# The first projection takes X before its norm; its units are scaled per token when they leave PSUM, and seven convolution taps go from VectorE to TensorE

## The chip, the cores and the metric

The kernel runs on one core of a Trainium2 chip, as one program with one launch. The metric is the device time in microseconds (us) of one execution; the time before is the median of three. The engines are TensorE (PE; its weight loads are PEld), VectorE (DVE), ScalarE (ACT), GpSimd (POOL) and SyncE (SP, which here only issues transfers). Each engine works through its own list of instructions in order and waits on semaphores.

## The reference

Two transformer blocks over 512 tokens of width 1024 in float32. The change lies in the first mixer of the first block. Its part of the reference, cut:

```python
def rmsnorm(x, g):
    y = x32 * lax.rsqrt(jnp.mean(x32 * x32, axis=-1, keepdims=True) + EPS)
    return (y * g).astype(x.dtype)

def conformer_conv(h, w_pw1, b_pw1, w_dw, b_dw, ln_g, ln_b, w_pw2, b_pw2):
    u = h @ w_pw1 + b_pw1                      # 1024 -> 2 x 1024
    a, gate = jnp.split(u, 2, axis=-1)
    u = a * jax.nn.sigmoid(gate)
    u = depthwise_conv(u, w_dw) + b_dw         # causal, 31 taps per channel
    u = jax.nn.silu(layernorm(u, ln_g, ln_b))
    return u @ w_pw2 + b_pw2

x = x + conformer_conv(rmsnorm(x, norm_mix[0]), ...)
```

After it come a feed-forward, dilated attention, a second feed-forward, and the second block. The factor of the norm is one number per token, so it can be applied to the rows of h or, after the product, to the rows of h @ w_pw1.

## The kernel before

All activations lie transposed: 128 channels on the partitions, 512 tokens along the row, so X is 8 tiles of 128x512. A product in float32 is made of three products of rounded parts: every operand is split into a high and a low part (`H_hi`, `H_lo`, `W_hi`, `W_lo`), high on ACT, low on DVE by a subtraction. Weights come in units of 256 columns (1 MB for `pw1`), through two buffers `W_raw`; a unit j is split into the buffer of unit j-2.

The first projection, `pw1`, has 8 units. Unit j gives, in two banks of PSUM, value tile j and gate tile j. Its 48 products run on PE in one go. Before unit 0 the token statistics are made: squares on ACT, sums on DVE, sums over channels on PE (`first_sum`, with filling products on zeros between them), the root on ACT, the reciprocal on DVE, and a spread of the four columns over a bank of PSUM on PE (`token_spread`). Then DVE makes the normed tiles (`normed`), ACT and DVE split them (`normed_hi`, `normed_lo`).

When unit j is done, ACT takes the sigmoid of the gate out of PSUM (`glu_gate(j)`), and DVE makes tile j of U as (value + bias) x gate, which also frees the banks (`glu_made`). Then ACT splits the high part of unit j+2 and DVE its low part (`split_hi`, `split_lo`); PE waits for it as `w_lo`. A unit's turn on DVE is called a round below.

The convolution of 31 taps runs on three engines at once, channel tile by channel tile. Tile 4 and the later taps of tile 6 are products with diagonal matrices on PE, behind the eight units (`conv_tap`); the diagonals are made by ACT in chunks of six taps (`diagonals`), and the input is split by ACT and by POOL (`conv_hi`, `conv_lo`). Tiles 2, 3, 7 and parts of 0 and 6 are multiply-adds on DVE, a fixed number behind each unit (`DVE_TAPS`). Tiles 1, 5 and the first taps of 0 are on POOL, which only adds; ACT multiplies the tap beforehand into one of 11 buffers (`scaled_tap`, `TAP`). The order in each list is written by hand: on ACT, behind the gate of the last unit, chunk 4 of the diagonals, four scaled taps, chunk 5, four taps, and so on; on POOL, `conv_lo(1)`, which tile 6 on PE waits for, stands ahead of tap 18 of tile 5. At the end PE sums the eight tiles over the channels for the mean of the layer norm, the last three of them tile 7 and tile 6 (DVE) and tile 5 (POOL).

Of the kernel before, what the change touches and what calls it, by code (L numbers as in the profile page):

```python
# [195 lines left out]
def build(nc, a, out):  # L196
# [14 lines left out]
    with ctx:  # L211
# [508 lines left out]
        def _(pe):  # L720
# [77 lines left out]
            def first_sum():  # L798

                for k in range(DT // 2):  # L800
                    pe.wait_ge(ss_made, k + 1)
                    for b in range(4):
                        last = nc.tensor.matmul(AUX[0][:, b:b + 1], tokens(FIRST_SQ[2 * k], b), ones[:, 0:1],
                                                start=(k == 0 and b == 0), stop=(k == DT // 2 - 1 and b == 3))
                    if k < DT // 2 - 1:
# [1498 lines left out]
        def _(dve):  # L2304
# [108 lines left out]
            for m in range(DT):  # L2413
                normed_lo(m)
                if m < DT - 2:
                    normed(m + 2)
# [900 lines left out]
```

## Time and profile before

| | |
|---|---|
| median of three executions | 1744.92 us (1744.68 to 1745.17) |
| the profiled execution | 1744.05 us, its span 1742.2 us |
| TensorE busy | 1713.0 us, 98% of the span |
| VectorE, ScalarE, GpSimd busy | 1205.4, 833.2 and 273.4 us |
| granted TensorE clock, mean | 0.996 of full speed |
| the stage of the change | 0 to about 151 us |

Times in the profile count from the start of the span. "Idle before" an instruction is the time its engine stood still ahead of it, with what ended the wait. A busy PE need not be a PE that sets the end: in the chain of work that ended last one sees which engine it was in each stretch.

### The profile page before, as it was taken

The numbers are of one execution on the slowest core, as the hardware profiler recorded it, in microseconds if no ns is written. First come the engines' busy times: TensorE is split into PE (matmuls) and PEld (weight loads), VectorE is DVE, ScalarE is ACT, GpSimd is POOL, SyncE is SP. The second block draws the span as 40 slices with busy tenths as digits, with TensorE's granted clock in tenths as the row PEclk, the third lists the DMA queues.
The fourth block names the chain that finished last, engine by engine and source line by source line (L and its number), as shares of the span: only waits on it lengthen the run. The fifth ranks groups of instructions, "written<-read, shape, count | busy, mean of one in ns | idle before, by whom it ended". The sixth has DMA issues, their size and how long they took to land.

```text
span 1742.2 us, 24232 instructions
## 1 busy us (share of the span) xinstructions
PE 1713.0 (98%) x9506; PEld 1430.2 (82%) x9506; DVE 1205.4 (69%) x1652; ACT 833.2 (48%) x1380; POOL 273.4 (16%) x207
## 2 busy tenths in 40 slices
PE   9999999999999999999999999999999999999998
PEld 6885889889988787799889988766678778888887
DVE  6998789549955555889459956569636676536753
ACT  6876555325633443556226534555654444214432
POOL 2994200000001000200000013672201200000002
PEclk9999999999999999999999999999999999999998
DMA  4210422312231311222412332422112123222321
GB/s 182 95 55 25 127 93 102 137 59 108 98 136 70 129 67 37 93 95 98 157 49 98 118 131 90 146 89 87 61 50 92 68 82 115 91 73 96 107 98 49
DMA packets 28948, 163.45 MB, mean 94 GB/s; under 512 B 4607, under 2 KB 7947, under 8 KB 12460
## 3 DMA queue, kind: packets, MB, share of 16 engines
q1 hardware_dynamic: 25664, 156.28, 25.3%
q10 hardware_dynamic: 3180, 5.74, 1.1%
q8 instruction: 70, 1.15, 0.3%
q14 instruction: 34, 0.28, 0.0%
HBM read 154.65 MB, written 4.47 MB: 91 GB/s over the span
## 4 chain that ended last, share of the span: by engine, by line
PE 84%; DVE 7%; POOL 6%; ACT 2%; issue 1%; DMA 0%; POOLq 0%; ACTq 0%; DVEq 0%
PE PSUM L738 19%; PE PSUM L740 18%; PE PSUM L739 18%; PE PSUM L1007 7%; PE PSUM L1008 7%; PE PSUM L1009 7%; POOL CV L2200 4%; DVE W_lo L2339 1%; POOL ISC L2264 1%; DVE WK L2930 1%; PE PSUM L1243 1%; PE PSUM L1264 1%; PE PSUM L1255 1%; PE PSUM L1094 0%; DVE H_lo L2312 0%
## 5 line engine op out<-in xcount | busy, mean ns | idle before, releaser
L738 PE MATMUL PSUM<-H_hi,W_hi 128*128 128x512 f32 x1056 | 426.0, 403 | 7.7 <-DVE W_lo L2339 2.9
L740 PE MATMUL PSUM<-H_hi,W_lo 128*128 128x512 f32 x1056 | 411.9, 390 | 0.0
L739 PE MATMUL PSUM<-H_lo,W_hi 128*128 128x512 f32 x1056 | 411.9, 390 | 0.0
L1449 ACT ACTIVATE W_hi<-W_raw 128x2048 fp32r<-128x2048 f32 (+1 forms) x96 | 181.9, 1895 | 318.9 <-PE PSUM L740 318.9
L2339 DVE TENSOR_TENSOR W_lo<-W_raw,W_hi 128x2048 fp32r<-128x2048 f32 (+1 forms) x96 | 237.3, 2472 | 71.8 <-ACT W_hi L1449 42.3
L2152 POOL TENSOR_TENSOR SSUM<-SSUM,SQ 128x512 f32<-128x512 f32 x43 | 62.5, 1454 | 1303.6 <-ACT SQ L1516 1301.8
L738 PEld LDWEIGHTS PSUM<-H_hi,W_hi 128*128 128x128 f32 x1056 | 198.3, 188 | 69.3 <-issue 21.2
L740 PEld LDWEIGHTS PSUM<-H_hi,W_lo 128*128 128x128 f32 x1056 | 198.2, 188 | 42.5
L739 PEld LDWEIGHTS PSUM<-H_lo,W_hi 128*128 128x128 f32 x1056 | 198.5, 188 | 37.2 <-issue 1.0
L738 PE MATMUL PSUM<-HID_hi,W_hi 128*128 128x512 f32 x480 | 187.3, 390 | 1.5 <-DVE HID_lo L2504 1.4
L739 PE MATMUL PSUM<-HID_lo,W_hi 128*128 128x512 f32 x480 | 186.8, 389 | 0.0
L740 PE MATMUL PSUM<-HID_hi,W_lo 128*128 128x512 f32 x480 | 186.7, 389 | 0.0
L738 PEld LDWEIGHTS PSUM<-HID_hi,W_hi 128*128 128x128 f32 x480 | 90.1, 188 | 21.7 <-issue 2.5
L740 PEld LDWEIGHTS PSUM<-HID_hi,W_lo 128*128 128x128 f32 x480 | 90.1, 188 | 18.8
L739 PEld LDWEIGHTS PSUM<-HID_lo,W_hi 128*128 128x128 f32 x480 | 90.1, 188 | 18.5
L1007 PE MATMUL PSUM<-E_hi,W_hi 128*128 128x256 f32 x272 | 77.0, 283 | 0.0
L1007 PE MATMUL PSUM<-E_hi,SLOT_hi 128*128 128x256 f32 x272 | 77.0, 283 | 0.0
L1009 PE MATMUL PSUM<-E_hi,W_lo 128*128 128x256 f32 x272 | 77.0, 283 | 0.0
L1008 PE MATMUL PSUM<-H_lo,W_hi 128*128 128x256 f32 x272 | 76.9, 283 | 0.0
L1007 PE MATMUL PSUM<-H_hi,W_hi 128*128 128x256 f32 x272 | 76.9, 283 | 0.0
L1009 PE MATMUL PSUM<-E_hi,SLOT_lo 128*128 128x256 f32 x272 | 76.9, 283 | 0.0
L1009 PE MATMUL PSUM<-H_hi,W_lo 128*128 128x256 f32 x272 | 76.8, 283 | 0.0
(412 smaller groups left out, 3475.5 us busy)
## 6 DMA issues: line engine op xcount, KB each, us to landing
W_raw<-in_inp SPq DMA_DIRECT2D x13, 1024.0 KB, 4.8
W_raw<-in_pw SPq DMA_DIRECT2D x11, 1024.0 KB, 4.8
W_raw<-in_gu0a SPq DMA_DIRECT2D x11, 1024.0 KB, 4.8
W_raw<-in_gu0b SPq DMA_DIRECT2D x11, 1024.0 KB, 4.8
W_raw<-in_gu1a SPq DMA_DIRECT2D x11, 1024.0 KB, 4.8
W_raw<-in_gu1b SPq DMA_DIRECT2D x11, 1024.0 KB, 4.8
W_raw<-in_gu2a SPq DMA_DIRECT2D x11, 1024.0 KB, 4.8
W_raw<-in_gu2b SPq DMA_DIRECT2D x11, 1024.0 KB, 4.8
```

Of the source, the lines that this page charges most:

```text
L738: nc.tensor.matmul(dst[:], wh, x_hi[:, k, :], start=(k == first), stop=False)
L739: nc.tensor.matmul(dst[:], wh, x_lo[:, k, :], start=False, stop=False)
L740: return nc.tensor.matmul(dst[:], wl, x_hi[:, k, :], start=False, stop=(k == last))
L1007: nc.tensor.matmul(dst, wh, xh, start=start, stop=False, skip_group_check=True)
L1008: nc.tensor.matmul(dst, wh, xl, start=False, stop=False, skip_group_check=True)
L1009: return nc.tensor.matmul(dst, wl, xh, start=False, stop=last, skip_group_check=True)
L1243: nc.tensor.matmul(S_BANK[i][:, 0:w], AQ[HD * i:HD * (i + 1), t, b * P:(b + 1) * P], KK[HD * i:HD * (i + 1), 0:w], start=True, stop=True). ...
L1255: last = nc.tensor.transpose(TO_BANK[:, c * P:(c + 1) * P], E2[:, i, c * P:(c + 1) * P], ident)
L1449: i = nc.scalar.activation(W_hi[b][:, 0:n], W_raw[b][:, 0:n], ACT.Copy)
L2152: nc.gpsimd.tensor_tensor(SSUM[:], SSUM[:], SQ[:, m.parity, :], ALU.add).then_inc(ss_made, 1)
L2200: nc.gpsimd.tensor_tensor(acc, acc, TAP[k % len(TAP)], ALU.add).then_inc(pool_tap, 1)
L2339: i = nc.vector.tensor_tensor(W_lo[b][:, 0:n], W_raw[b][:, 0:n], W_hi[b][:, 0:n].bitcast(F32), ALU.subtract)
```

## The change

Unit products now take X times the weight of the norm, without the token's factor. PE starts on unit 0 as soon as the first tile and half of the first weights are split. The squares, sums and root are made meanwhile; the two parts of `first_sum` and `token_spread` stand inside units 0 and 1 on PE, and DVE copies the spread factors into `R`. Each unit's value and gate are multiplied by `R` on DVE as they leave PSUM; the sigmoid works in place on the scaled gate in SBUF, and the last step of the round reads the scaled value from SBUF. One tap of the convolution stands between the gate's product and the wait for the sigmoid. Tile 6 starts on PE at tap 3 and not at tap 10; DVE keeps taps 0 to 2, POOL has the taps that it had. Transfers are issued in another order: X and weight tiles by turns on SP, the weights of the norm first on ACT's queue. The rest are counts of semaphores, and a tap buffer that takes the place of `R`.

```diff
-PE_TILES = [(4, 0), (6, 10)]
+PE_TILES = [(4, 0), (6, 3)]
-DVE_TILES = [(0, 8, CONV_WIDTH), (2, 0, CONV_WIDTH), (3, 0, CONV_WIDTH), (6, 0, 10), (7, 0, CONV_WIDTH)]
-DVE_TAPS = [12] * 7
+DVE_TILES = [(0, 8, CONV_WIDTH), (2, 0, CONV_WIDTH), (3, 0, CONV_WIDTH), (6, 0, 3), (7, 0, CONV_WIDTH)]
+DVE_TAPS = [10, 10, 9, 9, 9, 9, 9]
+TAPS_BESIDE_GATE = 1
...
-        TAP = [SQ[:, 0, :], SQ[:, 1, :], STD[:], T_hid[:], T_u[:], R[:]]
+        TAP = [SQ[:, 0, :], SQ[:, 1, :], STD[:], T_hid[:], T_u[:]]
...
+            first_tiles(0)
             sp.dma_start(W_raw[0][:, 0:FIRST_COLS], ...).then_inc(first_in, 16)
+            first_tiles(1)
             sp.dma_start(W_raw[0][:, FIRST_COLS:2 * FIRST_COLS], ...).then_inc(raw_in[0], 16)
+            first_tiles(2)
+            first_tiles(3)
...
-            zero_products(4)
-            pe.wait_ge(const_in, 16)
-            first_sum()
-            zero_products(1)
-            pe.wait_ge(r_made, MIX0 + 1)
-            token_spread(AUX[1], r_ps)
-            zero_products(3)
+            zero_products(5)
...
+                if k == 5:
+                    pe.wait_ge(const_in, 16)
+                    first_sum(0)
...
+                        if (j, half, k) == (1, 0, 0):
+                            first_sum(1)
+                        if (j, half, k) == (1, 0, 2):
+                            pe.wait_ge(r_made, MIX0 + 1)
+                            token_spread(AUX[1], r_ps)
...
             def glu_gate(j):
-                act.wait_ge(acc_ready, 2 * j + 2)
-                if j >= 2:
-                    act.wait_ge(glu_made, j - 1)
-                nc.scalar.activation(GATE[j % 2][:], PS[2 * (j % 2) + 1][:], ACT.Sigmoid, ...).then_inc(gate_act, 1)
+                act.wait_ge(glu_in, j + 1)
+                nc.scalar.activation(GATE[j % 2][:], GATE[j % 2][:], ACT.Sigmoid, ...).then_inc(gate_act, 1)
...
             for j in range(L.n):
+                value = U[:, j, HALO:HALO + SEQ]
+                dve.wait_ge(acc_ready, 2 * (L.base + j) + 1)
+                nc.vector.tensor_tensor(value, PS[2 * (j % 2)][:], R[:], ALU.mult).then_inc(glu_value, 1)
                 dve.wait_ge(acc_ready, 2 * (L.base + j) + 2)
+                nc.vector.tensor_tensor(GATE[j % 2][:], PS[2 * (j % 2) + 1][:], R[:], ALU.mult).then_inc(glu_in, 1)
+                conv(TAPS_BESIDE_GATE, j)
                 dve.wait_ge(gate_act, j + 1)
-                nc.vector.scalar_tensor_tensor(out=U[:, j, HALO:HALO + SEQ], in0=PS[2 * (j % 2)][:], scalar=vec("b_pw1", j),
+                dve.wait_ge(glu_value, VALUE0 + j + 1)
+                nc.vector.scalar_tensor_tensor(out=value, in0=value, scalar=vec("b_pw1", j),
                                                in1=GATE[j % 2][:], op0=ALU.add, op1=ALU.mult).then_inc(glu_made, 1)
```

On VectorE, one round of `pw1` before: the last step of unit 1, the low part of unit 3's weights, and taps (a tap is L2445; the first one waits for U). The number 128x512 is the tile that an instruction works on, the names in brackets the semaphores that it waits for.

```order
L2474 SCALAR_TENSOR_TENSOR U<-PSUM,vecs,T_g 128x512 [waits gate_act,acc_ready]
L2339 TENSOR_TENSOR W_lo_57<-W_raw_53,W_hi_55 128x2048 [waits w_hi]
L2445 SCALAR_TENSOR_TENSOR PSUM<-U,vecs,PSUM 128x512 [waits conv_step,acc_free]
L2445 SCALAR_TENSOR_TENSOR PSUM<-U,vecs,PSUM 128x512 [waits conv_step] x10
L2453 TENSOR_TENSOR CV<-CV,PSUM 128x512 [waits conv_step,pool_tap]
```

The same round on VectorE now (R holds the factors, T_g the gate, a tap is L2487):

```order
L2516 TENSOR_TENSOR U<-PSUM,R 128x512 [waits acc_ready]
L2518 TENSOR_TENSOR T_g<-PSUM,R 128x512 [waits acc_ready]
L2487 SCALAR_TENSOR_TENSOR PSUM<-U,vecs,PSUM 128x512 [waits conv_step]
L2522 SCALAR_TENSOR_TENSOR U<-U,vecs,T_g 128x512 [waits w_parts,gate_act]
L2366 TENSOR_TENSOR W_lo_57<-W_raw_53,W_hi_55 128x2048 [waits w_hi]
L2487 SCALAR_TENSOR_TENSOR PSUM<-U,vecs,PSUM 128x512 [waits conv_step,acc_free]
L2487 SCALAR_TENSOR_TENSOR PSUM<-U,vecs,PSUM 128x512 [waits conv_step] x9
```

Two products out of PSUM and one tap now stand ahead of the last step of the round, which reads U and not PSUM.

On ScalarE, the gates of units 6 and 7 (L1611) with what stands between them before: the high part of unit 8's weights, scaled taps for GpSimd, and the split of tile 6.

```order
L1611 ACTIVATE T_act<-PSUM,vecs 128x512 [waits acc_free,acc_ready]
L1449 ACTIVATE W_hi_54<-W_raw_52 128x2048 [waits acc_ready,raw_in0]
L1582 ACTIVATE SQ<-U,vecs 128x512 [waits pool_tap] x2
L1582 ACTIVATE STD<-U,vecs 128x512 [waits pool_tap]
L1592 ACTIVATE UP_hi<-U 128x542 [waits acc_free]
L1611 ACTIVATE T_g<-PSUM,vecs 128x512 [waits acc_free,acc_ready]
```

The same place on ScalarE now, where L1638 is the gate:

```order
L1638 ACTIVATE T_act<-T_act,vecs 128x512 [waits glu_in]
L1462 ACTIVATE W_hi_54<-W_raw_52 128x2048 [waits acc_ready,raw_in0]
L1611 ACTIVATE SQ<-U,vecs 128x512 [waits pool_tap] x2
L1611 ACTIVATE STD<-U,vecs 128x512 [waits pool_tap]
L1621 ACTIVATE UP_hi<-U 128x542 [waits acc_free]
L1638 ACTIVATE T_g<-T_g,vecs 128x512 [waits glu_in]
```

The order is the same; the gates now wait for VectorE's product (glu_in) where they waited for PE's unit (acc_ready).

## Rows read from the trace of the kernel before

**Rows 1.** The page: TensorE's busy time, share of the span, instructions.

```profile
PE 1713.0 (98%) x9506; PEld 1430.2 (82%) x9506; DVE 1205.4 (69%) x1652; ACT 833.2 (48%) x1380; POOL 273.4 (16%) x207
```

**Rows 2.** The chain that ended last: start us, us, engine, tile, line.

```profile
34.54 2.80 POOL CV L2200
...
128.26 1.37 POOL UP_lo L2168
...
147.75 3.45 PE PSUM L943 x8
```

**Rows 3.** Timeline of TensorE: start us, us, line, tiles, count, idle before.

```profile
31.16 0.49 PE L738 MATMUL PSUM<-H_hi,W_hi 128*128 128x512 f32 x1
...
107.44 0.39 PE L897 MATMUL PSUM<-UP_hi,D_hi 128*128 128x512 f32 x1
...
129.68 0.50 PE L897 MATMUL PSUM<-UP_hi,D_hi 128*128 128x512 f32 x1 [0.42 <-POOL UP_lo L2168]
...
146.73 1.02 PE L935 MATMUL PSUM<-SSUM,cmat 128*128 128x512 f32 x2
```

**Rows 4.** Timeline of the opening: products, splits and statistics of unit 0.

```profile
7.96 1.02 PE L803 MATMUL PSUM<-cmat,SSUM 128*128 128x1 f32 x8 [1.06 <-DMA cmat<-in_cmat]
...
14.43 1.05 ACT L1549 ACTIVATE W_hi<-W_raw 128x1024 fp32r<-128x1024 f32 x1
...
15.04 1.05 PE L817 MATMUL PSUM<-cmat,R 128*128 128x128 f32 x8
...
16.23 1.28 DVE L2392 TENSOR_TENSOR CV<-X,PSUM 128x512 f32<-128x512 f32 x2 [1.48 <-PE PSUM L817]
...
17.43 1.22 DVE L2410 TENSOR_TENSOR W_lo<-W_raw,W_hi 128x1024 fp32r<-128x1024 f32 x1
...
19.46 0.47 PE L738 MATMUL PSUM<-H_hi,W_hi 128*128 128x512 f32 x1 [0.79 <-DVE H_lo L2397]
```

**Rows 5.** DMA issues: tiles, count, KB each, median us from issue to landing.

```profile
W_raw<-in_pw SPq DMA_DIRECT2D x11, 1024.0 KB, 4.8
...
to_tokens<-in_to_tokens SPq DMA_DIRECT2D x1, 512.0 KB, 3.3
```

**Rows 6.** Timeline of VectorE in the rounds of units 0, 1 and 7.

```profile
32.17 0.75 DVE L2474 SCALAR_TENSOR_TENSOR U<-PSUM,vecs,T_act 128x512 f32<-128x512 f32 x1 [0.68 <-ACT T_act L1611]
33.88 2.29 DVE L2339 TENSOR_TENSOR W_lo<-W_raw,W_hi 128x2048 fp32r<-128x2048 f32 x1 [0.95 <-ACT W_hi L1449]
...
37.40 6.67 DVE L2445 SCALAR_TENSOR_TENSOR PSUM<-U,vecs,PSUM 128x512 f32<-128x512 f32 x10
...
44.88 3.24 DVE L2339 TENSOR_TENSOR W_lo<-W_raw,W_hi 128x2048 fp32r<-128x2048 f32 x1 [0.15 <-ACT W_hi L1449]
...
114.35 0.74 DVE L2474 SCALAR_TENSOR_TENSOR U<-PSUM,vecs,T_g 128x512 f32<-128x512 f32 x1
...
145.35 0.69 DVE L2456 TENSOR_TENSOR CV<-CV,PSUM 128x512 f32<-128x512 f32 x1
```

**Rows 7.** VectorE's seven splits of weights in the rounds, busy time together.

```profile
33.20:107.00 73.80, 18.88 (x7) 1.00 0.27 98
```

**Rows 8.** Timeline of ScalarE: a split, the last gate, chunk 4, the taps behind.

```profile
31.94 1.91 ACT L1449 ACTIVATE W_hi<-W_raw 128x2048 fp32r<-128x2048 f32 x1
...
107.64 0.69 ACT L1611 ACTIVATE T_g<-PSUM,vecs 128x512 f32<-128x512 f32 x1 [1.52 <-PE PSUM L740]
...
111.83 0.40 ACT L1603 ACTIVATE D_hi<-cmat,tap_hi 128x128 fp32r<-128x128 f32 x1 [3.51 <-PE PSUM L899]
...
115.37 0.71 ACT L1582 ACTIVATE T_hid<-U,vecs 128x512 f32<-128x512 f32 x1
```

**Rows 9.** Timeline of GpSimd: first tap, two first taps of tile 1, tile 5's tap 13.

```profile
33.24 0.77 POOL L2181 TENSOR_SCALAR CV<-U,vecs 128x512 f32<-128x512 f32 x1 [31.67 <-DVE U L2474]
...
46.17 4.13 POOL L2181 TENSOR_SCALAR CV<-U,vecs 128x512 f32<-128x512 f32 x2 [0.20 <-POOL CV L2200]
...
121.64 1.30 POOL L2200 TENSOR_TENSOR CV<-CV,T_hid 128x512 f32<-128x512 f32 x1
```

More of the change, by code:

```diff
@@ L796, in zero_products, with first_sum @@
                     nc.tensor.matmul(PS[2][:], ZERO[:, 0:P], ZERO[:], start=True, stop=True)
[L798 to L805, printed above, removed]
-                        zero_products(1)
-                last.then_inc(stat_ready, 1)
+            def first_sum(part):
+                pe.wait_ge(ss_made, (3, 6)[part])
+                for b in range(4):
+                    last = nc.tensor.matmul(AUX[0][:, b:b + 1], tokens(FIRST_SQ[(0, 4)[part]], b), ones[:, 0:1],
+                                            start=(part == 0 and b == 0), stop=(part == 1 and b == 3))
+                if part:
+                    last.then_inc(stat_ready, 1)
             def idle_products(bank, n):
@@ L925, in _ @@
                     for k in range(L.kt):
+                        if (j, half, k) == (1, 0, DT // 2):
+                            pe.wait_ge(w_lo, 2)
                         last = product(j % 2, L, half, k, H_hi, H_lo)
@@ new lines, in _ @@
+            first_square(1)
+            act.wait_ge(x_in[1], 16)
+            first_hi(2)
+            first_hi(3)
+            act.wait_ge(raw_in[0], 16)
+            first_weights(0, 1, w_hi)
+            first_square(2)
+            first_square(3)
+            act.wait_ge(x_in[2], 16)
+            first_hi(4)
+            first_hi(5)
+            first_square(4)
+            act.wait_ge(x_in[3], 16)
+            first_hi(6)
+            first_hi(7)
+            act.wait_ge(raw_in[1], 16)
+            first_weights(1, 0, w_half)
@@ L2398, in normed_lo, with first_w_lo, first_pair @@
                                                in1=H_hi[:, m, :].bitcast(F32), op0=ALU.mult, op1=ALU.subtract).then_inc(h_lo_made, 1)
-            for k in range(DT // 2):
+            def first_w_lo(u, half, made):
+                cols = slice(half * FIRST_COLS, half * FIRST_COLS + FIRST_COLS)
+                nc.vector.tensor_tensor(W_lo[u][:, cols], W_raw[u][:, cols], W_hi[u][:, cols].bitcast(F32),
+                                        ALU.subtract).then_inc(made, 1)
+            def first_pair(k):
@@ new lines, in _ @@
+            first_pair(0)
+            first_h_lo(2)
+            first_h_lo(3)
+            dve.wait_ge(w_hi, 1)
+            first_w_lo(0, 1, w_lo)
+            first_pair(1)
+            first_h_lo(4)
+            first_h_lo(5)
+            two_pairs(0, 2)
+            first_h_lo(6)
+            first_h_lo(7)
+            dve.wait_ge(w_half, 2)
+            first_w_lo(1, 0, first_lo)
+            first_pair(2)
+            first_pair(3)
+            two_pairs(2, 5)
+            dve.wait_ge(w_hi, 2)
@@ L2403, in _ @@
+            first_w_lo(1, 1, w_lo)
             dve.wait_ge(std_made, MIX0 + 1)
             nc.vector.reciprocal(R4[:], STD4[:]).then_inc(r_made, 1)
[L2405 to L2411 removed]
@@ L2412, in _ @@
[L2412 to L2421 removed]
+            dve.wait_ge(r_ps, TOKEN_NORMS.index(MIX0) + 1)
@@ L2422, in _ @@
+            nc.vector.tensor_copy(R[:], AUX[1][:]).then_inc(r_copied, 1)
+            dve.wait_ge(r_copied, COPIED_NORMS.index(MIX0) + 1)
             dve.wait_ge(vec_in, 16)
```

90 lines of the change are left out of this document (40 added, 50 removed).

## The prediction

> **What bounds the kernel now.** The page comes first: TensorE is busy 98% of the span [rows 1], which invites the thought that only work taken off it can help. The chain that ended last says otherwise for the stage of the change: from 34.54 to 128.26 us its pieces are GpSimd's taps of the convolution, then the split `conv_lo(1)`, 128.26 + 1.37 = 129.63 us, and only from there TensorE, up to 151.20 us [rows 2]. TensorE's timeline shows why: the seven units behind unit 0 run without a gap, (107.44 - 31.16) / 7 = 10.90 us each; 31 taps of tile 4 follow at (129.68 - 0.42 - 107.44) / 31 = 0.704 us; then it stands 0.42 us for `conv_lo(1)`, starts tile 6 at 129.68 and is through at 146.73 [rows 3]. Its own work and GpSimd's meet within half a microsecond. VectorE is third: it has tile 7 at 145.35 + 0.69 = 146.04 [rows 6]. So three engines end together, and what I need of each is when it starts and how fast its turns go.
>
> **The start.** Before, PE took its first product at 19.46: first the sums and the spread (until 16.09), then VectorE's products with the factor, and only then the splits [rows 4]. Now X needs no norm. A lone transfer of 512 KB lands 3.3 us after its issue, and one of 1024 KB after 4.8 [rows 5], so a second 512 KB in the same queue costs 1.5 us: with an issue at 0.7 us, X lands at 4.0, the first half of the weights at 5.5. The high part (1.05) and the low part (1.22) of that half [rows 4] take it to 7.9; PE starts at 8.0, behind its five filling products. Pairs of X tiles land at 4.0, 7.0, 10.0 and 11.5, with the halves of the weights between; PE works 2.7 us on a pair (10.9 / 4) from 8.0 on, so none should be late. Unit 0 with the first sum (1.02 [rows 4]) ends at 8.0 + 10.9 + 0.95 = 19.8. In unit 1 follow 0.7 of products, the second sum 0.95, two steps of 1.4 that cover the root and the reciprocal, and the spread, 1.05: 23.8. Copying R out of PSUM I price like the product that reads PSUM, 0.68 (two of them take 1.28 [rows 4], so 0.60 from start to start), two small splits of the taps 0.5: at 25.0 VectorE begins round 0. Value and gate 1.28, sigmoid with its two hand-overs 0.9, last step 0.74: tile 0 of U is there at 27.9 instead of 32.17 + 0.75 = 32.92 [rows 6]. **Gain at the start: 5.0 us**, which GpSimd gets at its first tap (33.24 [rows 9]), and 11.3 us for PE's units (19.8 against 31.16), less 2.0 for sum and spread inside unit 1.
>
> **The round on VectorE.** Here the change adds a wait. Before, ScalarE had the gate as soon as PE ended a unit, and its high part of the next weights was mostly ready when VectorE wanted it; only in round 0, where both ran at PE's heels, VectorE stood 0.95 us for it, and 0.15 in round 1 [rows 6]. Now the gate waits for VectorE's product, and behind the gate on ScalarE stand the high part of unit j+2, the taps for GpSimd and the diagonals for PE. From the end of the gate's product: 0.1 to hand over (between engines it took 0.03, from 31.94 + 1.91 to 33.88, and 0.14, from 16.09 to 16.23 [rows 4, 6, 8]), 0.6 from the gate's start to the split's, as from start to start of two such instructions above, 1.91 for the split [rows 8]; at +2.6 VectorE may start the low part. Its own work till then, one tap (0.66) and the last step (0.74), is 1.4; the rest it stands. The low part took 18.88 / 7 = 2.70 [rows 7]. Ten taps take 6.67, so one is (6.67 - 0.74) / 9 = 0.66 [rows 6], and 65 taps over seven rounds are 6.13 a round. With value and gate of the next unit, 1.28: 2.6 + 2.62 + 6.13 + 1.28 = **12.63 us a round**, where before the seven from 32.17 to 114.35 took 11.74 with the joins of tiles 0 and 2 [rows 6]. Those are three additions of 0.69 with a hand-over each, 2.15. From gate product 0 at 26.3 the one of unit 7 is at 26.3 + 7 x 12.63 + 2.15 = 116.9, and U's last tile at 118.5, 3.4 us later than before (115.09) in spite of the start. PE is now paced as well: unit 7 starts on the low part of round 5, at about 26.3 + 5 x 12.63 + 1.4 + 5.2 = 96, and ends at 107, as before; the 9.3 us that it had won are spent in waits for `w_lo`.
>
> **What is late next.** ScalarE's list has the gate of unit 7 ahead of chunk 4 of the diagonals and of the tap that GpSimd adds as tap 13 of tile 5. Before, that gate ran at 107.64, chunk 4 from 111.83 to 115.37, and GpSimd took tap 13 at 121.64 with the tap long in its buffer [rows 8, 9]. Now the gate ends at 117.7, chunk 4 (3.54) at 121.2, the scaled tap (0.71) at 121.9: GpSimd gets tap 13 at 122.1. Its 5.0 us are gone. Five taps took it from 121.64 to 128.26; chunk 5, another 3.5 on ScalarE behind four scaled taps, makes tap 17 wait some 0.6 more, so `conv_lo(1)` comes at 129.3 instead of 128.26: **+1.0 us**.
>
> **Seven taps.** Tile 6 on PE starts at 130.7 and has 28 taps instead of 21: 7 x 0.704 = **+4.9 us**, all behind `conv_lo(1)` on the chain. Its end moves from 146.73 to 146.73 + 1.0 + 4.9 = 152.7, and the sums behind it from 151.20 to 157.1. VectorE, with 47 taps at 0.66 and three joins (2.2) after U's last tile, has tile 7 at 151.7, or at 152.7, since the same count gives 1.0 too little for before; it is wanted for the third sum, two sums of 3.45 / 4 = 0.86 [rows 2] behind 152.7, at 154.4, so it hides. The seven taps that VectorE loses (4.6) only help it to be hidden. Chunk 9 of the diagonals (five taps, about 2.9 on ScalarE) lies beside 23 taps of PE.
>
> **Edits at nothing.** Squares, pair sums and the root lie beside unit 0 (PE's 10.9 us cover some 8 of them); if PE had to wait there, each microsecond would shift round 0 and so the end one for one. The other tap buffer, the counts and `COPIED_NORMS` move no work. The clock is 1.00 in the rounds [rows 7]; I take no change in it. Everything behind the mean shifts as a whole. **Sum: +1.0 + 4.9 = +5.9 us**, from 1744.05 us of the profiled execution (span 1742.2) to 1750.0. The median before, 1744.92, stands 0.87 above that execution; the forecast for the median is 1750.8.
>
> **What the rows don't show.** The sigmoid out of SBUF: out of PSUM it took 0.69, a scaled tap out of SBUF 0.71 [rows 8]; I take 0.69. The low part, 2.29 with GpSimd idle and 3.24 beside it [rows 6]; I take the mean of the seven. The landing of X and weights by turns, a microsecond either way, which shifts everything. Round times from 12.1 to 13.2 move gate 7 by -3.7 to +4.0, and the end as far: +2.1 to +9.9.
>
> **The port.** The last step of a round read PSUM and SBUF, now it reads two tiles of SBUF, as the low part does. The low part at 44.88 and two GpSimd taps at 46.17 stretched each other: 3.24 against 2.29, and 4.13 for two taps of 0.77 [rows 6, 9]. The Trainium skill has the rule in "SBUF — State Buffer", section "Who interferes with whom": a VectorE instruction with two inputs in SBUF and a GpSimd instruction that reads SBUF exclude each other for the whole instruction. The trace agrees: the tap ends where the low part ends plus its own 0.77. By these rows GpSimd could lose up to 0.74 in each of seven rounds, 5.2 us, and VectorE up to a tap's 1.30 a round. If nothing covered GpSimd's loss, the sum would be 5.9 + 5.2 = 11.1. I leave it at 5.9: VectorE's loss lies in its wait for the split, and GpSimd's in the 5.0 us that it wins and then waits for tap 13.
>
> **Rivals.** (1) The change does what PE's rows alone would suggest: rounds keep up, `conv_lo(1)` is never late, and PE sets the end: -11.3 + 2.0 + 4.9 = -4.4, 1740.5 us. It needs `conv_lo(1)` 9.3 us earlier, while GpSimd starts only 5.0 earlier with the same taps. Against it stands the chain [rows 2]. Chance 0.06, for a GpSimd that loses much less to the low parts than before. (2) The round trip is hidden, gate product 7 comes before 111.5 and GpSimd never waits for a tap (116.6 less 5.1 for gate, chunk and tap; rounds under 11.9): then `conv_lo(1)` is 5.0 earlier at best and the seven taps cost 4.9: 0, up to +3; 1745 to 1748. What speaks for it is that my round is only 0.8 over that point. Chance 0.20. (3) The port's loss is not hidden: up to 5.2 more, +8 to +11, 1753 to 1756. Chance 0.08. (4) The forecast, +3 to +8: 0.66.
>
> **Numbers.** Two tenths of a percent, 3.5 us, is about what a measurement of this kernel tells from no change. The forecast reaches into "same" with 0.05. Faster 0.06, same 0.20 + 0.04 = 0.24, slower 0.70. The range, 1746.5 to 1755, holds the forecast, the upper half of (2) and most of (3).
>
> **What would show it.** Right: U's first tile near 28 us; VectorE standing about a microsecond for the split in most rounds, PE 1 to 3 us for `w_lo` ahead of units 4 to 7; ScalarE's gate 7 near 117 after a long wait for VectorE; GpSimd's tap 13 waiting for ScalarE; tile 6 on PE from about 130.7. Wrong: gate 7 before 111.5, or `conv_lo(1)` before 126 (then rival 2), or a first product on PE well after 8 us, which would add to the sum.

## The result, and the profile after

The changed kernel takes 1752.18 us (median of 6 runs, 1752.05 to 1753.57) beside 1745.05 (1744.35 to 1745.39) for the kernel before: a ratio of 1.0043 with a 95% interval from 1.0031 to 1.0055. That is 7.1 us slower; the forecast was 5.9 us slower, 1750.8. In the two profiled executions the spans are 1750.7 and 1742.2.

The page after: busy time of the engines, then the chain that ended last, by engine.

```profile
PE 1713.0 (98%) x9499; PEld 1430.2 (82%) x9499; DVE 1213.4 (69%) x1657; ACT 837.9 (48%) x1395; POOL 275.1 (16%) x207
...
PE 84%; DVE 9%; ACT 4%; issue 2%; POOL 1%; DMA 0%; SPq 0%; DVEq 0%; POOLq 0%; ACTq 0%
```

TensorE is busy for 1713 us as before [rows 1], but not with the same work: the seven taps have come in, and half of the filling products on zeros in the opening have gone (6.3 us instead of 12.7). So the 8.5 us that the span has grown can't be read off its busy time. GpSimd's taps, which the chain ran through before [rows 2], have nearly left it (GpSimd has 6% of the chain before, 1% now), and VectorE and ScalarE stand in it instead (7% and 2% before). VectorE's timeline after (start us, us, line, tiles, count, idle before); L2518 is the gate's product with R, L2522 the last step of a round, L2366 the low part of the weights:

```profile
26.68 0.68 DVE L2518 TENSOR_TENSOR T_act<-PSUM,R 128x512 f32<-128x512 f32 x1
...
28.15 0.75 DVE L2522 SCALAR_TENSOR_TENSOR U<-U,vecs,T_act 128x512 f32<-128x512 f32 x1 [0.79 <-ACT T_act L1638]
29.96 2.29 DVE L2366 TENSOR_TENSOR W_lo<-W_raw,W_hi 128x2048 fp32r<-128x2048 f32 x1 [1.05 <-ACT W_hi L1462]
...
40.82 1.80 DVE L2522 SCALAR_TENSOR_TENSOR U<-U,vecs,T_g 128x512 f32<-128x512 f32 x1
42.62 2.29 DVE L2366 TENSOR_TENSOR W_lo<-W_raw,W_hi 128x2048 fp32r<-128x2048 f32 x1
...
117.50 0.68 DVE L2518 TENSOR_TENSOR T_g<-PSUM,R 128x512 f32<-128x512 f32 x1
...
118.97 0.77 DVE L2522 SCALAR_TENSOR_TENSOR U<-U,vecs,T_g 128x512 f32<-128x512 f32 x1
```

U's first tile is there at 28.90 (before 32.92) and its last at 119.74 (before 115.09 [rows 6]): 4.0 us earlier at the start, 4.65 later at the end of the rounds. A round takes (117.50 - 26.68) / 7 = 12.97 us. The rows show two faces of one delay. In round 0 the low part waits 1.05 us for ScalarE; in round 1 it waits for nothing, but the step before it takes 1.80 us instead of 0.75.

ScalarE's timeline after, at the last gate, then GpSimd's at its first tap, at tap 12 of tile 5 and from tap 13 to `conv_lo(1)`, and last GpSimd's tap 12 in the kernel before:

```profile
118.21 0.72 ACT L1638 ACTIVATE T_g<-T_g,vecs 128x512 f32<-128x512 f32 x1 [7.76 <-DVE T_g L2518]
```

```profile
29.22 0.77 POOL L2208 TENSOR_SCALAR CV<-U,vecs 128x512 f32<-128x512 f32 x1 [27.65 <-DVE U L2522]
...
120.85 1.29 POOL L2227 TENSOR_TENSOR CV<-CV,STD 128x512 f32<-128x512 f32 x1
123.52 1.30 POOL L2227 TENSOR_TENSOR CV<-CV,T_hid 128x512 f32<-128x512 f32 x1 [1.37 <-ACT T_hid L1611]
...
129.48 1.29 POOL L2227 TENSOR_TENSOR CV<-CV,TAP 128x512 f32<-128x512 f32 x1 [0.71 <-ACT TAP L1611]
130.73 1.34 POOL L2195 TENSOR_TENSOR UP_lo<-U,UP_hi 128x542 fp32r<-128x542 f32 x1
```

```profile
120.19 1.30 POOL L2200 TENSOR_TENSOR CV<-CV,STD 128x512 f32<-128x512 f32 x1
```

Gate 7 comes 10.6 us later than before [rows 8]; chunk 4 and the scaled tap (`T_hid`) that GpSimd waits for stand behind it, and GpSimd, which had started 4.0 us earlier than before, has tap 13 1.9 us later and `conv_lo(1)` 2.5 us later [rows 2, 9]. TensorE's timeline after, at the first product, at tile 6 and at the sums, and a row of its waits in the rounds (us in total, times, longest):

```profile
8.96 0.50 PE L746 MATMUL PSUM<-H_hi,W_hi 128*128 128x512 f32 x1 [1.23 <-DVE W_lo L2424]
...
132.12 0.49 PE L904 MATMUL PSUM<-UP_hi,D_hi 128*128 128x512 f32 x1 [1.76 <-POOL UP_lo L2195]
...
146.75 0.50 PE L904 MATMUL PSUM<-UP_hi,D_hi 128*128 128x512 f32 x1 [0.28 <-ACT D_lo L1632]
...
155.08 1.02 PE L948 MATMUL PSUM<-SSUM,cmat 128*128 128x512 f32 x2
```

```profile
PE PSUM L746 <- DVE W_lo L2366: 8.1, 5, 2.5
```

The sums begin at 155.08 instead of 146.73 [rows 3], 8.35 us later, and the span is 8.5 longer: everything behind the mean has only been shifted.

The chain that ended last, in this stretch (start us, us, engine, tile, line):

```profile
119.20 0.40 ACT D_hi L1632
...
151.13 0.30 ACT D_lo L1632
151.47 0.50 PE PSUM L904
```

From chunk 4 of the diagonals to the end of chunk 9 it stays on ScalarE, 32 us of diagonals and scaled taps, and only the last five taps of tile 6 and the sums are TensorE's. Neither GpSimd's tap 13 nor `conv_lo(1)` is in it. (Just ahead of 119.20 the profile names a matmul of TensorE's tile 4. But in run 4, with chunk 4 ahead of the gate and tile 4 at the same time, chunk 4 begins at 112.84: what holds it here is the gate.)

### The profile page after: what moved, and what is told of

Same layout as the page of the kernel before. It is cut to its first block, busy times and chain, and to the rows that moved or that the text cites. A ratio compares the mean times of both kernels' runs of the same rounds, so it can differ in the third digit from the quotient of the medians.

```text
span 1750.7 us, 24232 instructions
## 1 busy us (share of the span) xinstructions
PE 1713.0 (98%) x9499; PEld 1430.2 (82%) x9499; DVE 1213.4 (69%) x1657; ACT 837.9 (48%) x1395; POOL 275.1 (16%) x207
## 4 chain that ended last, share of the span: by engine, by line
PE 84%; DVE 9%; ACT 4%; issue 2%; POOL 1%; DMA 0%; SPq 0%; DVEq 0%; POOLq 0%; ACTq 0%
PE PSUM L746 19%; PE PSUM L748 19%; PE PSUM L747 19%; PE PSUM L1020 7%; PE PSUM L1021 7%; PE PSUM L1022 6%; DVE PSUM L2487 2%; DVE W_lo L2366 1%; ACT W_hi L1462 1%; POOL ISC L2291 1%; ACT D_hi L1632 1%; ACT D_lo L1632 1%; DVE WK L2978 1%; PE PSUM L1256 1%; PE PSUM L1277 0%
## 5 line engine op out<-in xcount | busy, mean ns | idle before, releaser
L2366 DVE TENSOR_TENSOR W_lo<-W_raw,W_hi 128x2048 fp32r<-128x2048 f32 (+1 forms) x95 | 235.1, 2474 | 72.9 <-ACT W_hi L1462 43.4
```

What stands on the lines that cost most here:

```text
L2366: i = nc.vector.tensor_tensor(W_lo[b][:, 0:n], W_raw[b][:, 0:n], W_hi[b][:, 0:n].bitcast(F32), ALU.subtract)
```

## The experiments

Differences between kernels are taken through the kernel before as it ran beside each: the changed kernel stands 7.1 us above it.

**1. The seven taps alone, in the kernel before**

```diff
-PE_TILES = [(4, 0), (6, 10)]
+PE_TILES = [(4, 0), (6, 3)]
```

VectorE's list of tiles follows (tile 6 ends at tap 3).

> The kernel before with one part of the change alone: TensorE takes tile 6 from tap 3 instead of tap 10 and VectorE does three of its taps instead of ten; everything else is as before. Theory (the seven taps stand behind GpSimd's UP_lo, at 0.70 us each, and nothing on TensorE gives the time back): +4.9 us, about 1750.0. Rival A (TensorE's taps are hidden, since the mean sums wait for another engine): 1745, no change, and the whole loss of the changed kernel belongs to the scaling. Rival B (the extra chunk of diagonals holds up ScalarE's scaled taps and so GpSimd as well): above +6, about 1752.

Measured 1749.82 us beside 1744.90, ratio 1.0026 (1.0015 to 1.0037): +4.9. TensorE's timeline, tile 6, the sums and the first squares behind them:

```profile
129.74 0.50 PE L897 MATMUL PSUM<-UP_hi,D_hi 128*128 128x512 f32 x1 [0.49 <-POOL UP_lo L2168]
...
151.66 1.02 PE L935 MATMUL PSUM<-SSUM,cmat 128*128 128x512 f32 x2
...
157.65 1.95 PE L951 MATMUL PSUM<-SQ,cmat 128*128 128x512 f32 x4 [1.54 <-ACT SQ L1656]
```

The start of tile 6 stays (129.68 before [rows 3]) and the sums move by 4.93, as 7 x 0.704 says. Both rivals fall.

**2. The changed kernel without the seven taps on TensorE**

```diff
-PE_TILES = [(4, 0), (6, 3)]
+PE_TILES = [(4, 0), (6, 10)]
```

> The changed kernel without its seven taps on TensorE: tile 6 is split at tap 10 as before, the rest of the change stays. Theory: TensorE's taps end near 150.3 instead of 155.2, but VectorE, which ends its tile 7 at 153.3 in the changed kernel, now does seven more taps of 0.67 us and ends at 158.0; the sum of tile 7 and the two behind it then take 2.6, so the subtraction begins at about 160.7 instead of 159.6: 1753.3, one us more than the changed kernel. Rival A (the seven taps are pure loss): 1752.2 - 4.9 = 1747.3. Rival B (VectorE's extra taps find idle time): 1752, as the changed kernel.

Measured 1755.96 beside 1744.90, ratio 1.0065 (1.0052 to 1.0079): 11.1 us above the kernel before, 4 more than the changed kernel and not 1.1. VectorE ended where expected, but the sums behind it took twice their time. TensorE's timeline, and the granted clock there (window, length, busy, clock, DMA share, GB/s):

```profile
157.95 5.49 PE L956 MATMUL PSUM<-CV,cmat 128*128 128x512 f32 x6 [6.92 <-DVE CV L2498]
```

```profile
158.00:163.00 5.00, 5.00 (x6) 0.50 0.00 0
```

A sum's matmul took 5.49 / 6 = 0.92 us, where eight take 3.45 before [rows 2], 0.43 each: TensorE stood 6.92 us and then ran at a granted clock of 0.50, the lower of its two levels (1.2 GHz). The same six take 2.84 us in run 4, so 2.65 of the 4 us are the clock's, and the rest is VectorE's later end, as expected. So in the changed kernel the seven taps on TensorE are no loss: they keep VectorE's tile 7 from being the end.

**3. `conv_lo(1)` earlier on GpSimd**

```diff
-                    if (m, t) == (5, 18):
+                    if (m, t) == (5, 10):
                         conv_lo(1)
```

> The changed kernel with one step of GpSimd moved: UP_lo of tile 6 is made before tap 10 of tile 5 instead of before tap 18, about 10 us earlier; its input UP_hi has been there since 110.4. Theory (TensorE's second tile waits for this step alone, 1.76 us, and everything behind it follows): TensorE begins tile 6 at 130.4 instead of 132.1, all of the end moves by 1.7: 1750.5. Rival A (chunk 5 of the diagonals, ScalarE's, is as late): less than 0.5, about 1752. Rival B (VectorE's tile 7 or GpSimd's last tap takes over as the end, at 153.3 and 152.1): about 1 us, 1751.2.

Measured 1752.63 beside 1744.90, ratio 1.0048 (1.0034 to 1.0061): no gain. The wait for UP_lo is gone, and two things stand in its place in the profiled execution. TensorE's timeline of this run, behind one of its waits for the weights, at the start of tile 4 and in tile 6:

```profile
71.24 0.80 PE L746 MATMUL PSUM<-H_hi,W_hi 128*128 128x512 f32 x1 [2.54 <-DVE W_lo L2366]
71.84 0.63 PE L747 MATMUL PSUM<-H_lo,W_hi 128*128 128x512 f32 x1
...
110.00 0.39 PE L904 MATMUL PSUM<-UP_hi,D_hi 128*128 128x512 f32 x1
...
146.60 0.50 PE L904 MATMUL PSUM<-UP_hi,D_hi 128*128 128x512 f32 x1 [0.69 <-ACT D_lo L1632]
```

Matmuls took 0.63 us instead of 0.39 for some 3 us after a wait of 2.54, and again after one of 1.87 at 97.39. The first fall was taken up by the next wait (0.48 us instead of 1.89); behind the second, tile 4 began at 110.0 instead of 108.5. But even without it little was to be won: TensorE then waits for ScalarE's diagonals, and the tap behind that wait starts at 146.60, where it started at 146.75 in the changed kernel. The sums begin 0.15 us earlier (154.93). That is rival A, though the chunk that is late is 8 and not 5. My theory that UP_lo alone holds tile 6 falls for tile 6's end.

**4. Chunk 4 and four scaled taps ahead of the last gate on ScalarE**

```diff
             for j in range(L.n):
+                if j == L.n - 1:
+                    diagonals(CHUNK_BUFS)
+                    scaled_taps(PRODUCTS_BEHIND)
                 glu_gate(j)
```

> The changed kernel with two steps of ScalarE changing places: the diagonals of chunk 4 and the four scaled taps behind them are issued ahead of the last gate instead of after it (the gate's input comes at 118.2, and ScalarE stood idle for 7.76 us before it). Theory (the gate that waits for VectorE's product holds up what GpSimd wants): tap 13 of tile 5 no longer waits 1.37 us nor tap 17 0.71, UP_lo of tile 6 begins at 128.7 instead of 130.7, TensorE's tile 6 at 130.2 instead of 132.1: 1750.4. Rival A (GpSimd waits for its own additions, and ScalarE's order has no part): 1752.2. Rival B (the gate is now late itself and moves VectorE's tile 7 by as much as was won): 1752 or more.

Measured 1751.03 beside 1744.90, ratio 1.0039 (1.0025 to 1.0052): 6.1 us, 1.0 less than the changed kernel, where 1.8 were expected (the two intervals overlap; the executions don't, 1750.27 to 1751.80 against 1752.05 to 1753.57). TensorE's and VectorE's timelines:

```profile
130.47 0.51 PE L904 MATMUL PSUM<-UP_hi,D_hi 128*128 128x512 f32 x1 [0.21 <-POOL UP_lo L2199]
...
152.38 1.02 PE L948 MATMUL PSUM<-SSUM,cmat 128*128 128x512 f32 x2
...
154.75 2.84 PE L956 MATMUL PSUM<-CV,cmat 128*128 128x512 f32 x6 [0.50 <-DVE CV L2502]
```

```profile
119.57 1.54 DVE L2526 SCALAR_TENSOR_TENSOR U<-U,vecs,T_g 128x512 f32<-128x512 f32 x1 [0.81 <-ACT T_g L1638]
```

Tile 6 starts 1.65 us earlier and TensorE reaches the sums 2.7 earlier, without a wait for a diagonal: the last gate's place in ScalarE's list did hold up both GpSimd and TensorE. Part of it goes to rival B: VectorE waits 0.81 for the gate, its last step is stretched, and then the sums wait 0.50 for tile 7.

**5. Without the scaling**

The two products of a round with R are left out; gate and last step read PSUM.

```diff
-                nc.vector.tensor_tensor(value, PS[2 * (j % 2)][:], R[:], ALU.mult).then_inc(glu_value, 1)
-                nc.vector.tensor_tensor(GATE[j % 2][:], PS[2 * (j % 2) + 1][:], R[:], ALU.mult).then_inc(glu_in, 1)
-                nc.vector.scalar_tensor_tensor(out=value, in0=value, scalar=vec("b_pw1", j),
+                nc.vector.scalar_tensor_tensor(out=value, in0=PS[2 * (j % 2)][:], scalar=vec("b_pw1", j),
```

> The changed kernel without the scaling itself: the two products with R in each round are left out, the gate's sigmoid and the last step read PSUM as before, so the first projection's units are not normed and the output is not the reference's; the new start, the taps and everything else stay. It prices the 16 products and what they bring on. Theory (the rounds lose 1.2 us each by the products and by the round trip, and that is all that eats the early start): rounds of 11.7 us as before, started 4.0 earlier, so UP_lo of tile 6 comes 4.0 earlier than in the kernel before, near 124.5, and the time is that of the kernel before with the seven taps, less 4.0: 1745.8. Rival A (TensorE sets the end anyhow, as the mean sums follow its 59 taps): with the units done by about 104, the same 1745 to 1746, but TensorE waits for nothing in tile 6. Rival B (the rounds are longer because GpSimd's additions now lie beside VectorE from the start, not because of the products): rounds stay near 12.5 and the time above 1749.

Measured 1745.39 beside 1744.29, ratio 1.0006 (0.9996 to 1.0015). VectorE's last steps of rounds 0 and 7:

```profile
26.11 0.74 DVE L2520 SCALAR_TENSOR_TENSOR U<-PSUM,vecs,T_act 128x512 f32<-128x512 f32 x1
...
100.22 0.74 DVE L2520 SCALAR_TENSOR_TENSOR U<-PSUM,vecs,T_g 128x512 f32<-128x512 f32 x1
```

A round takes (100.22 - 26.11) / 7 = 10.59 us. The time is as the theory had it, though the rounds are shorter than its 11.7, since they hold ten or eleven taps where before there were twelve. Rival A falls, since TensorE waits 3.4 us for `conv_lo(1)`, and rival B with the rounds. Scaling costs 12.97 - 10.59 = 2.38 us a round, and the two products take only 1.2 of it (each begins 0.60 after the one ahead).

**6. The split ahead of the gate on ScalarE**

```diff
-                glu_gate(j)
                 if j < L.n - 1:
                     split_hi(act, L, At(j))
+                glu_gate(j)
```

> The changed kernel with ScalarE splitting the next weights (W_hi) ahead of the gate instead of behind it, since the split waits for nothing that VectorE's gate product makes. Theory (the split sits behind a gate that now waits for VectorE: 2.6 us of waits for W_hi over the seven rounds, and TensorE's waits for W_lo of up to 2.5 us follow from it): the last gate product comes near 115.5 instead of 117.5, tap 13 of GpSimd waits for nothing, UP_lo of tile 6 is 1.4 to 2 us earlier, 1750.3; and where TensorE's clock fell to its lower level behind its two longest waits for W_lo (in the runs of three variants of this kernel, not in the profiled run of the changed kernel itself), it stays at the upper one. Rival A (the gate itself now comes 1.9 us later and VectorE waits for it instead): 1752, no change. Rival B (VectorE's last step, stretched beside GpSimd, takes up what is won): less than 1 us, 1751.5.

Measured 1752.70 beside 1744.29, ratio 1.0050 (1.0036 to 1.0064): nothing won, and rival B. VectorE's timeline, round 5 and the last gate product:

```profile
79.35 1.86 DVE L2523 SCALAR_TENSOR_TENSOR U<-U,vecs,T_act 128x512 f32<-128x512 f32 x1
81.13 3.38 DVE L2367 TENSOR_TENSOR W_lo<-W_raw,W_hi 128x2048 fp32r<-128x2048 f32 x1
...
117.57 0.68 DVE L2519 TENSOR_TENSOR T_g<-PSUM,R 128x512 f32<-128x512 f32 x1
```

No low part waits for ScalarE any more, but six of the seven take 3.35 to 3.39 us instead of 2.28. VectorE waits for the gate in round 0 alone (0.79 us, as in the changed kernel), so rival A falls. TensorE's clock did stay at its upper level, behind a wait for `w_lo` that had grown to 3.32 us (last section).

**7. The scaled value written back to PSUM**

```diff
+                scaled = PS[2 * (j % 2)][:]
-                nc.vector.tensor_tensor(value, PS[2 * (j % 2)][:], R[:], ALU.mult).then_inc(glu_value, 1)
+                nc.vector.tensor_tensor(scaled, PS[2 * (j % 2)][:], R[:], ALU.mult).then_inc(glu_value, 1)
-                nc.vector.scalar_tensor_tensor(out=value, in0=value, scalar=vec("b_pw1", j),
+                nc.vector.scalar_tensor_tensor(out=value, in0=scaled, scalar=vec("b_pw1", j),
```

> The changed kernel with the scaled value written back to its PSUM bank, so that the last step of a round reads PSUM and SBUF as in the kernel before, and not SBUF twice. In the changed kernel that step takes 1.47 to 1.87 us in five rounds of eight, while GpSimd adds, and 0.75 to 0.79 in three. Theory P (what stretches it is two operands in SBUF beside GpSimd's additions): 0.75 in all rounds, 4.9 us less on VectorE by the last round, the last gate product near 113.5, 1749 or a little less. Rival A (it is stretched by GpSimd whatever it reads): steps as long as before, 1752. Rival B (the steps are short, but the weights' split or the taps beside GpSimd are stretched in their place, or ScalarE's W_hi is waited for longer): gate product at 116 to 117, 1751.5.

Measured 1751.87 beside 1744.29, ratio 1.0044 (1.0030 to 1.0059): nothing again, and again rival B. VectorE's timeline, round 1 and the last gate product, then its waits for W_hi (us in total, times, longest):

```profile
40.61 0.75 DVE L2523 SCALAR_TENSOR_TENSOR U<-PSUM,vecs,T_g 128x512 f32<-128x512 f32 x1
42.42 2.53 DVE L2366 TENSOR_TENSOR W_lo<-W_raw,W_hi 128x2048 fp32r<-128x2048 f32 x1 [1.05 <-ACT W_hi L1462]
...
116.78 0.68 DVE L2519 TENSOR_TENSOR T_g<-PSUM,R 128x512 f32<-128x512 f32 x1
```

```profile
DVE W_lo L2366 <- ACT W_hi L1462: 7.4, 7, 1.1
```

All eight last steps take 0.75, and what they gave back is waited away: 1.05 us for W_hi in every round, 7.4 in all, against 2.6 in the changed kernel.

**8 and 9. Both, with chunk 4's diagonals ahead of the last gate, and both alone**

Edits 6 and 7 together; run 8 also moves `diagonals(CHUNK_BUFS)`, without the scaled taps, ahead of the last gate.

> The changed kernel with three edits at once: the split of the weights ahead of the gate, the scaled value written back to PSUM, and the diagonals of chunk 4 ahead of the last gate (the scaled taps stay behind it). Theory (the round trip and the stretched step are most of what the rounds lose, chunk 4 the rest, and each of the three is on the path): last gate product near 112, UP_lo of tile 6 near 126, TensorE's second tile right behind its first: 1747 to 1748, still above the kernel before, since 4.9 us of taps stay. Rival A (VectorE's tile 7 becomes the end): 1749. Rival B (they don't add up, the same wait is counted twice): 1750.

> The changed kernel with two edits at once, the split of the weights ahead of the gate and the scaled value written back to PSUM; ScalarE's chunk 4 stays behind the last gate. Each of these two edits alone gave nothing, and the three together gave 8 us. Theory (either edit alone lets the other's delay come up in its place: with the split behind the gate VectorE waits 1.05 us a round for W_hi; with it ahead, the split's lower half or the last step, both operands in SBUF, waits as long for GpSimd): rounds of 11.7 us as with the three, the last gate product near 108.7, and with ScalarE at the last gate 9 us earlier chunk 4 no longer holds up GpSimd: 1744.7. Rival A (chunk 4's place is what was missing in the two single edits): rounds of 11.7, but GpSimd waits for its taps again and the time is 1746 to 1747. Rival B (the gain came of an interplay with chunk 4 on TensorE): 1750.

Measured: the three 1744.71 beside 1744.29, ratio 1.0004 (0.9994 to 1.0013); the two 1745.68 beside 1744.22, ratio 1.0006 (0.9997 to 1.0016). VectorE's first and last gate product in the run of two:

```profile
26.57 0.68 DVE L2520 TENSOR_TENSOR T_act<-PSUM,R 128x512 f32<-128x512 f32 x1
...
108.59 0.68 DVE L2520 TENSOR_TENSOR T_g<-PSUM,R 128x512 f32<-128x512 f32 x1
```

Rounds of (108.59 - 26.57) / 7 = 11.72 us: the two edits, each worth nothing, are worth 1.25 us a round together. The two stand 1.5 us above the kernel before, the three 0.4: 5.7 and 6.7 of the 7.1 are gone, more than I had expected of the three (1747 to 1748). The two intervals overlap, and in the run of two GpSimd waits for no tap of ScalarE's (rival A), so chunk 4's place is worth nothing sure once ScalarE reaches the last gate 9 us earlier. And with the scaling left out (run 5) the time was 1.1 above, 0.4 less than with the two edits and inside the intervals: what the sixteen products add to a round, 11.72 against 10.59 us, hardly shows in the time.

**10. GpSimd nearly silent, with the split ahead of the gate**

```diff
-                    nc.gpsimd.tensor_tensor(acc, acc, TAP[k % len(TAP)], ALU.add).then_inc(pool_tap, 1)
+                    nc.gpsimd.tensor_tensor(acc[:, 0:1], acc[:, 0:1], TAP[k % len(TAP)][:, 0:1], ALU.add).then_inc(pool_tap, 1)
```

> The changed kernel with the split of the weights ahead of the gate, and GpSimd's scaled additions done on one column of 512 only (so its conv tiles are left incomplete and the output is not the reference's): same instructions and waits, but GpSimd is nearly always done at once. Theory P (VectorE's instructions with two operands in SBUF wait for GpSimd's additions): every last step takes 0.75 us, every W_lo 2.3 instead of 3.4, rounds of 11.7 us, the last gate product near 108.7. Rival (they are stretched by ScalarE's writes or by the landing of the weights): W_lo stays at 3.35 to 3.39 us in the rounds from the second on, and the last step at 1.3 to 1.9. The end of the stage says nothing here, since GpSimd's share of it is gone.

One run, 1742.21 us. VectorE's last steps of the odd rounds and its seven low parts (ns shortest/median/longest, first and last start); the last steps of the even rounds have 752/753/756:

```profile
L2523 DVE SCALAR_TENSOR_TENSOR U<-U,vecs,T_g x4: 751/752/753, 40.4 to 108.9; 128x512 f32<-128x512 f32 x4
...
L2367 DVE TENSOR_TENSOR W_lo<-W_raw,W_hi x7: 2281/2284/2287, 29.5 to 98.7; 128x2048 fp32r<-128x2048 f32 x7
```

With the same operands as in run 6, none is stretched: it was GpSimd's additions that VectorE waited for. The rival falls.

**11. A variant meant to beat both**

Run 8 with `conv_lo(1)` as in run 3, and tile 6 split at tap 5 instead of 3.

> The three edits of the run of three, and two more: UP_lo of tile 6 is made before tap 10 of tile 5 (GpSimd), and tile 6 is split at tap 5 instead of 3, so that VectorE, which stood still for 3.0 us at the end in the run of three, takes two taps back from TensorE. Theory (TensorE's end is what the end follows, and it waited 2.0 us for UP_lo): TensorE's taps end 2.0 + 1.4 us earlier, near 143.8, VectorE's tile 7 at 145.9, so the last sums end 3 us earlier: 1741.5, below the kernel before. Rival A (GpSimd's last tap, which ended at 145.3, and the one sum behind it set the end): still 1741.5, since that sum comes last. Rival B (as with UP_lo moved by itself, the diagonals or a fall of TensorE's clock eat it): 1744.

Measured 1742.65 beside 1744.22, ratio 0.9989 (0.9980 to 0.9998): 1.6 us less than the kernel before. VectorE's subtraction behind the sums, and the granted clock in a later window:

```profile
148.71 4.87 DVE L2538 SCALAR_TENSOR_TENSOR CV<-PSUM,CV 128x512 f32<-128x512 f32 x8 [2.21 <-PE PSUM L956]
```

```profile
1148.71:1168.71 20.00, 18.12 (x74) 0.91 0.30 88
```

The stage ends 3.0 us earlier than in run 8 (151.72), as expected; the span is only 1.4 shorter. In the profiled execution TensorE's clock fell a thousand microseconds later, in a stage that no edit touches, and in the same stretch of run 8's it stayed at 1.00: 9% of 20 us is 1.8. (Both fell once more, to 0.91, 200 us further on.)

**12. Two of the edits in the kernel before**

Edits 6 and 3.

> The kernel before with two of the edits that it can take too: the split of the weights ahead of the gate, and UP_lo of tile 6 ahead of tap 10. It asks whether the gain of the best variant belongs to the new start or to the edits. Theory (in the kernel before these two delays hardly stand on the path: VectorE waits 1.3 us for W_hi in all, TensorE 0.42 for UP_lo, and every last step takes 0.75): at most 0.5 to 1 us less, 1743.5 to 1744, so the best variant stays about 1 us ahead. Rival A (the edits are worth as much here): 1742.5 or less, and the new start is worth nothing. Rival B (the gate comes later behind the split and VectorE waits for it): 1746 or more.

Measured 1749.05 beside 1744.51, ratio 1.0022 (1.0011 to 1.0032): slower, rival B. VectorE's last step in round 0, then TensorE at the last sums and the squares behind them:

```profile
33.84 0.75 DVE L2475 SCALAR_TENSOR_TENSOR U<-PSUM,vecs,T_act 128x512 f32<-128x512 f32 x1 [2.58 <-ACT T_act L1611]
```

```profile
151.69 1.15 PE L943 MATMUL PSUM<-CV,cmat 128*128 128x512 f32 x2 [2.24 <-POOL CV L2187]
154.38 3.75 PE L951 MATMUL PSUM<-SQ,cmat 128*128 128x512 f32 x4 [1.54 <-ACT SQ L1657]
```

In the kernel before the gate waits for TensorE alone, so the split ahead of it only makes VectorE wait longer (2.58 instead of 0.68 [rows 6]); U's first tile is 1.67 later, GpSimd's last addition 2.1, and TensorE, idle for 2.24 us, then takes 3.75 us for four matmuls where experiment 1 took 1.95. Two of the eight executions took 1746.6 at a mean granted clock of 0.996, the others 1748.8 to 1749.3 at 0.994: by this about 2.5 of the 4.5 us would be the clock's and not come every time, though no trace shows those two executions. Edit 3 alone was not tried there; its wait is 0.42 us. So the best variant's gain doesn't come from edits that help either kernel, but how much of the 1.6 us is the start's stays open.

## Why the prediction was right

**The mechanism held as far as the last gate.** The early start is spent in the rounds, the gate's product holds ScalarE, and gate 7 comes 10.6 us late. Of the signs named ahead, these are in the trace after: a wait of 7.76 us ahead of gate 7, 1.37 us ahead of tap 13, waits for `w_lo` of 1.5 to 2.5 us ahead of units 4 to 7. The microsecond for the split came in two rounds and not in most.

**Behind the gate the path was another, and that the number fits is in part luck.** I had the chain run from the gate through chunk 4, GpSimd's tap 13 and `conv_lo(1)` into TensorE's 28 taps. The chain that ended last runs through ScalarE's list. The step that was wrong is "Chunk 9 of the diagonals ... lies beside 23 taps of PE": I put it at nothing without adding up that list. Its window from 131 to 154 us in the changed kernel (window, length, busy, clock, DMA share, GB/s) has no gap left:

```profile
131.00:154.00 23.00, 23.00 (x62) 1.00 0.00 0
```

Tile 6 took 151.66 - 129.74 = 21.92 us in run 1. From 132.12 on it would have ended at 154.04, so the path that I named ends 1.0 us before the real one, 155.08. The two lie close, and so the sum came out. In run 3, with `conv_lo(1)` out of the way, the end stays where it was (154.93). Run 1 has the same chunk 9 and no wait for it, since ScalarE reaches its last gate early there: both, the late gate and the longer list, make it late.

**The start was over-sized by 1.0 us.** U's first tile gained 4.0, not 5.0. TensorE's first product came at 8.96 instead of 8.0, behind the low part of the first weights, and the rest of the opening took as long as reckoned. That was one of the signs of being wrong that I had named, and it added to the sum as said there.

**The round was right.** Reckoned: 12.63 and 2.15 / 7 of joins, 12.94; measured 12.97. The low part starts 2.60 us behind the gate's product, as reckoned: 26.68 + 0.68 = 27.36 to 29.96 in round 0, and 2.60 in each of the seven. What fills the time was not all a wait of about 1.2 us for the split. It came so in two rounds (1.05 and 1.02); in five the last step was stretched instead, by 0.7 to 1.1, and at most 0.34 of the wait was left beside it.

**GpSimd.** The forecast let its loss lie in the wait ahead of tap 13, and most of it did: from its first tap to the end of tap 12 it took 92.9 us (29.22 to 122.14) instead of 88.3 (33.24 [rows 9] to 121.49). These 4.7 us, 3.0 of them new waits for VectorE and ScalarE in the rounds, were more than the 4.0 that it had won, before ScalarE's late tap made it wait 1.37 more. So a punctual tap 13 alone would not have brought `conv_lo(1)` back: in run 4, where it waits for no such tap, tile 6 still starts at 130.47 and not at 129.68.

**The port.** I left GpSimd's and VectorE's exclusion at nothing because it would lie in the wait for the split. Run 7 confirms that as far as it goes: unstretched steps alone won nothing. What I didn't see is the converse, that the wait for the split also lies in the exclusion, so that either cure alone fails and only both work (runs 8 and 9). The Trainium skill ("SBUF — State Buffer", "Who interferes with whom") says that a VectorE instruction with two inputs in SBUF contends with a GpSimd instruction that reads SBUF, and one with at most one such input doesn't; runs 7 and 10 agree with both halves (0.75 us with one input in PSUM, 0.75 with two in SBUF and GpSimd silent, up to 1.87 otherwise). One reading of mine was wrong: beside the low part of 2.29 us at 33.88 GpSimd was not idle. Its addition at 34.54 took 2.80 us [rows 2] where others take 1.30 [rows 9], and ended 1.17 behind the low part. There the low part had come first, and GpSimd paid.

**Seven taps: +4.9, measured +4.9** (run 1). But they stand for more than a loss: with VectorE's rounds as slow as they are, taking them back costs 4 (run 2).

**What the sum lacked.** `conv_lo(1)` was 1.4 us later than forecast (1.0 of the start, 0.4 behind it), and from 132.12 on TensorE needed 22.96 us for tile 6, where the forecast's 17.05 + 4.93 is 21.98: the 1.0 is mostly the waits for ScalarE's chunks 8 and 9, ahead of the taps at 146.75 and 151.47. Together 2.4, and 5.9 + 2.4 = 8.3 is the shift of the sums in the profiled execution. By the medians the loss is 7.1; the profiled execution before lay 1.0 under the median of 1745.05, the one after 0.3 over its own.

**The clock.** "I take no change in it" held for the profiled execution of the changed kernel. In those of three variants, runs 2 to 4, the clock fell in the rounds (last section); what it did in the changed kernel's other five executions no trace shows.

**The rivals.** (2), the round trip hidden, needed gate product 7 before 111.5. Runs 8 and 9 are that case made by hand (108.6): 1744.7 and 1745.7, inside the 1745 to 1748 given for it, or 0.3 under. (1), TensorE setting the end at 1740.5, nothing reached. (3), the port's loss on top, isn't what the kernel shows, since GpSimd still had to wait for ScalarE at tap 13, though the measured loss is near its lower end. (In the chances, the part of the forecast that reaches into "same" stands once as 0.05 and once as 0.04; the sums use 0.04.)

## What to carry to other kernels

Before an operand moves from PSUM to SBUF, look whether GpSimd is reading SBUF then; and before an engine's turn gets a round trip, look what stands behind the waiting instruction in the other engine's list. Where two delays lie side by side, each experiment on one alone reads as "no effect": try the pair before writing either off. And add up every engine's list in the stretch that a change fills, ScalarE's too, since an engine with a share of 48% over the span can be full where it counts. When the time comes out as forecast, still read the chain that ended last: it may be another one.

## What the hardware showed that I had not expected

TensorE's granted clock fell behind waits of 2.5 us, and did not behind the same waits in other runs. Its window of 72 to 76 us (length, busy, clock, DMA share, GB/s) in the profiled execution of run 3, behind a wait for `w_lo` of 2.54 us (at 71.24); then in that of the changed kernel, behind one of 2.53; then in that of run 6, with the matmul that ends the wait:

```profile
72.00:76.00 4.00, 4.00 (x15) 0.72 0.75 264
```

```profile
72.00:76.00 4.00, 4.00 (x19) 1.00 0.74 264
```

```profile
71.48 0.50 PE L746 MATMUL PSUM<-H_hi,W_hi 128*128 128x512 f32 x1 [3.32 <-DVE W_lo L2367]
```

```profile
72.00:76.00 4.00, 4.00 (x19) 1.00 0.76 262
```

Behind waits of 2.53 or 2.54 us the clock of this window was 0.62 in run 2, 0.72 in run 3 and 0.57 in run 4, and 1.00 in the changed kernel and in run 7; behind 3.32 us in run 6 it was 1.00 as well. So such waits cost their own time and, in some executions, more: tile 4 of run 3 began 1.5 us later. The runs show that it comes and goes, and not what decides it.
